# One decoder trunk on one core: seven quarter products in place of eight for the attention's queries and keys, too

## The reference, cut to what matters

```python
h = rms_norm(x, norm_mix[l])
proj = h @ w_in[l]                       # (256 x 1024) @ (1024 x 3584)
hq, hf, hi, hgate, aq, ak, av = jnp.split(proj, IN_SPLITS, axis=-1)   # 512 columns each
y_hg = hgrn2_mixer(hq, hf, hi, hgate, lbs[l], hg_out_norm[l])
y_att = dilated_attention_mixer(aq, ak, av, positions)
#   in it: qh = rope(heads(q), positions) * ATT_DH ** -0.5; kh = rope(heads(k), positions)
#   rope: concatenate([t1 * cos - t2 * sin, t2 * cos + t1 * sin]) of the halves t1, t2 of each head
x = x + jnp.concatenate([y_hg, y_att], axis=-1) @ w_out[l]
x = x + memory_cross_attention(rms_norm(x, norm_cross[l]), rms_norm(mem, norm_mem[l]), wq_x[l], wkv_x[l], wo_x[l])
x = x + hierarchical_moe(rms_norm(x, norm_ffn[l]), ...)
```

## Time and profile before

| | us |
|---|---|
| median of 3 runs (lowest, highest) | 1067.57 (1065.05, 1068.66) |
| the profiled execution | 1068.05 |
| its span | 1065.8 |
| TensorE busy (share of the span) | 1024.3 (96%) |
| VectorE busy | 413.5 (39%) |
| ScalarE busy | 135.6 (13%) |
| GpSimd busy | 98.4 (9%) |
| DMA, mean rate over the span | 275 GB/s |

### The profile page before, as it was taken

How to read it: one execution, slowest core, us unless ns; L and a number is a source line. 1 busy time by engine, 2 the same in 40 slices (tenths; PEclk the granted TensorE clock), 3 DMA queues, 4 the chain that set the end, 5 groups by cost and what they waited for, 6 DMA issues and landing times.

```text
span 1065.8 us, 10641 instructions
## 1 busy us (share of the span) xinstructions
PE 1024.3 (96%) x4360; PEld 549.1 (52%) x4360; DVE 413.5 (39%) x734; ACT 135.6 (13%) x307; POOL 98.4 (9%) x123
## 2 busy tenths in 40 slices
PE   6999999999998999999999999999999999999996
PEld 5757556567564543333333855565864433333332
DVE  2523375622143243332443636473032434444433
ACT  2211001412010011001112000041020011111111
POOL 2051032000001000000000512210000100000000
PEclk9999999999999999999999999999999999999999
DMA  9943001954038899999999520078463699999994
GB/s 359 424 175 141 17 0 69 417 229 157 1 158 339 353 395 422 415 423 421 418 422 419 223 79 1 0 305 346 162 237 123 241 422 421 421 421 421 421 422 179
DMA packets 43673, 293.58 MB, mean 275 GB/s; under 512 B 5344, under 2 KB 5600, under 8 KB 10848
## 3 DMA queue, kind: packets, MB, share of 16 engines
q1 hardware_dynamic: 36848, 266.35, 61.3%
q10 hardware_dynamic: 5616, 22.24, 5.3%
q0 software_dynamic: 1152, 4.19, 1.0%
HBM read 283.33 MB, written 9.44 MB: 275 GB/s over the span
## 4 chain that ended last, share of the span: by engine, by line
PE 89%; DVE 3%; DMA 3%; ACT 1%; SPq 1%; issue 1%; POOL 0%; DVEq 0%; POOLq 0%; ACTq 0%
PE bank L879 19%; PE bank L707 10%; PE bank L935 10%; PE bank L528 9%; PE bank L518 8%; PE bank L546 5%; PE bank L548 5%; PE bank L940 5%; PE bank L614 5%; PE bank L636 3%; DMA ring<-in_w_experts 3%; PE bank L508 2%; SPq L469 1%; PE bank L759 1%; PE bank L772 1%; PE bank L788 1%
## 5 line engine op out<-in xcount | busy, mean ns | idle before, releaser
L879 PE MATMUL bank<-ring,hT 128*64 128x512 f32 x704 | 182.8, 594 | 0.1
L707 PE MATMUL bank<-ring,hT 128*128 128x512 f32 x256 | 112.1, 594 | 0.0
L879 PEld LDWEIGHTS bank<-ring,hT 128*64 128x64 f32 x704 | 57.8, 137 | 93.8 <-issue 92.8
L528 PE MATMUL bank<-hT,ring 128*128 128x256 f32 x448 | 97.4, 379 | 0.8 <-DVE hT L1431 0.8
L1725 DVE TENSOR_TENSOR x<-bank,x 128x512 f32<-128x512 f32 x64 | 44.3, 692 | 137.5 <-PE bank L940 137.5
L528 PEld LDWEIGHTS bank<-hT,ring 128*128 128x128 f32 x448 | 84.9, 190 | 12.8 <-issue 1.4
L518 PE MATMUL bank<-ring,hT 128*128 128x512 f32 x192 | 84.4, 592 | 0.0
L707 PEld LDWEIGHTS bank<-ring,hT 128*128 128x128 f32 x256 | 48.0, 190 | 57.7 <-issue 56.8
L935 PE MATMUL bank<-ring,Vx 128*64 128x512 f32 x208 | 58.0, 596 | 2.7 <-ACT Vx L1167 2.4
L940 PE MATMUL bank<-PT 128*128 128x512 f32 x128 | 59.2, 605 | 0.0
L935 PE MATMUL bank<-ring,work 128*64 128x512 f32 x256 | 56.8, 596 | 2.2 <-ACT work L1167 2.2
(11 more groups left out here) (270 smaller groups left out, 1294.4 us busy)
## 6 DMA issues: line engine op xcount, KB each, us to landing
ring<-in_w_experts SPq DMA_DIRECT2D x160, 1024.0 KB, 13.9
ring<-in_w_mix SPq DMA_DIRECT2D x60, 1024.0 KB, 16.3
late<-in_w_experts SPq DMA_DIRECT2D x12, 1024.0 KB, 20.8
keys<-in_w_experts SPq DMA_DIRECT2D x10, 1024.0 KB, 20.4
work<-in_w_experts SPq DMA_DIRECT2D x10, 1024.0 KB, 24.1
late<-in_w_mix ACTq DMA_DIRECT2D x4, 2048.0 KB, 11.1
rot<-by_slot ACTq DMA_DIRECT2D x14, 512.0 KB, 8.0
by_slot<-late ACTq DMA_DIRECT2D x1, 4096.0 KB, 38.7
```

Source lines behind the costliest of these rows:

```text
L528: last = nc.tensor.matmul(b[:, k * T:(k + 1) * T], w[:, c, (n2 + k) * P:(n2 + k + 1) * P], rhs[:, c, :], start=(c == 0), stop=(c == C - 1))
L707: last = nc.tensor.matmul(held[name[1:], n, m][:, :], hT[:, c, m * P:(m + 1) * P], w[:, c, :], start=(c == 0), stop=(c == C - 1))
L879: last = nc.tensor.matmul(banks[2 + g][b2 * CAP:(b2 + 1) * CAP, :], rows_T_of(p)[:, c, b2 * CAP:(b2 + 1) * CAP], w, start=(c == 0), stop=( ...
```

## The change: what it does

aq and ak are computed by seven quarter products n1 to n7, with the same sums of rows as m1 to m7. m4 moves from behind the levels into the filling of level 4, with n1. GpSimd forms m4's weights in one subtraction of 128x2048 ahead of the levels; behind m5 it forms two more sums (in the slot SUMS, whose last use is now n4) and a third behind level 0's product of K, and n4's weights in pieces behind the products of levels 4 and 5's index (two pieces each). ScalarE copies n1 twice. VectorE adds the others into `rot` in SBUF and rotates there: `rotate` reads SBUF in place of the banks, sines first. The rotations end in the order of `TURNS`, and so go the transposes; s0 waits for qT1 in place of kT1.

```diff
+TURNS = [("qT", 0), ("kT", 1), ("kT", 0), ("qT", 1)]
 FIRST_SEVENTHS = [("m1", "A"), ("m2", "D")]
-BETWEEN = [[("m6", "D"), ("m5", "D")], [("m7", "D"), ("m3", "D")], [("hg0", "D")], [("hg1", "D")],
-           [("aq0", "D")], [("aq1", "D")], [("ak0", "D")], [("ak1", "D")]]
+BETWEEN = [[("m6", "D"), ("m5", "D")], [("m7", "D"), ("m3", "D")], [("hg0", "D")], [("hg1", "D")], [("m4", "D"), ("n1", "A")],
+           [("n2", "D"), ("n6", "D")], [("n5", "D"), ("n7", "D")], [("n3", "D"), ("n4", "D")]]
...
-    jobs += [("m4", "D")] + [(f"{name}{m}", "A") for name in ("qT", "kT") for m in range(M)]
+    jobs += [(f"{name}{m}", "A") for name, m in TURNS]
...
-LAST_USE = {"hf": "hf1", "hq": "hq1", "hi": "m4", "av": "m3", SUMS: "m5", "aq": "aq1", "ak": "ak1", "hg": "hg1",
+LAST_USE = {"hf": "hf1", "hq": "hq1", "hi": "m4", "av": "m3", SUMS: "n4", "aq": "n4", "ak": "n3", "hg": "hg1",
...
                 def seventh(name):
+                    one, two, late_sums = ("hi", "av", 4) if name[0] == "m" else ("aq", "ak", 11)
+                    t = 0 if name[0] == "m" else 4
                     rows_at, sums_at, weights, weights_at = {
+                        "1": (rows_block(0, 0), 0, weight_block(L, one, 0), 0), "2": (rows_block(0, 1), 0, weight_block(L, one, 1), 0),
+                        "5": (token_sums(0), 1, weight_block(L, SUMS, 0), t + 1), "6": (token_sums(1), 2, weight_block(L, SUMS, 1), t + 2),
+                        "7": (token_sums(2), 3, weight_block(L, two, 0), t + 3), "3": (token_sums(3), 4, weight_block(L, two, 1), 0),
+                        "4": (rows_block(1, 1), 0, weight_block(L, one, 0), late_sums)}[name[1]]
...
-                seventh("m4")
-                for w, name in enumerate(("qT", "kT")):
-                    for m in range(M):
-                        pe.wait_ge(rot_done, 4 * L + 2 * w + m + 1)
...
+                for i, (name, m) in enumerate(TURNS):
+                    pe.wait_ge(rot_done, 4 * L + i + 1)
+                    rr = turned(("qT", "kT").index(name), m)
+                    transposes(L, f"{name}{m}", [rr[:, k * P:(k + 1) * P] for k in range(4)])
...
+                wait_job(act, L, "n1")
+                nc.scalar.activation(turned(0, 1), bank("n1")[:, :], ACT.Copy)
+                empty("n1", turned(0, 0))
...
+                wait_job(pool, L, "m1")
+                weight_sums(minus(b11, b21, t2, ALU.subtract))
+                pool.wait_ge(weight_sum, 11 * L + 4)
+                c11, c21, c12, c22 = (weight_block(L, name, k) for name in ("aq", "ak") for k in range(2))
...
+                wait_job(pool, L, "m5")
+                weight_sums(minus(t1, c12, c11, ALU.subtract))
+                pool.wait_ge(weight_sum, 11 * L + 5)
+                weight_sums(minus(t2, c22, t1, ALU.subtract))
+                pool.wait_ge(weight_sum, 11 * L + 6)
                 for j in range(7):
...
-                    if 1 <= j <= 4:
-                        wait_job(pool, L, "m1")
-                        weight_sums(minus(b11[:, j - 1, :], b21[:, j - 1, :], t2[:, j - 1, :], ALU.subtract))
+                    if j == 0:
+                        weight_sums(minus(c12, c22, c12, ALU.subtract))
+                        pool.wait_ge(weight_sum, 11 * L + 7)
+                    if j in (4, 5):
+                        wait_job(pool, L, "n1")
+                        for c in (2 * j - 8, 2 * j - 7):
+                            weight_sums(minus(c11[:, c, :], c21[:, c, :], t2[:, c, :], ALU.subtract))
...
                 def rotate(w, m):
-                    name = f"{('aq', 'ak')[w]}{m}"
-                    wait_job(dve, L, name)
-                    t = bank(name)[:, :].rearrange("p (h u i) -> p h u i", u=2, i=32)
...
-                    V.tensor_tensor(r, t, cs, ALU.mult)
-                    emptied(V.tensor_tensor(b, t, sn, ALU.mult))
-                    wait_emptied(dve, L, name)
+                    link(V.tensor_tensor(b, r, sn, ALU.mult))
+                    link(V.tensor_tensor(r, r, cs, ALU.mult))
                     V.tensor_tensor(r[:, :, 0, :], r[:, :, 0, :], b[:, :, 1, :], ALU.subtract)
                     V.tensor_tensor(r[:, :, 1, :], r[:, :, 1, :], b[:, :, 0, :], ALU.add).then_inc(rot_done, 1)
...
+                def sum_seventh(name):
+                    of = name[0]
+                    one0, two0, one1, two1 = (hi[:, 0, :], av[:, 0, :], hi[:, 1, :], av[:, 1, :]) if of == "m" else \
+                        (turned(0, 0), turned(1, 0), turned(0, 1), turned(1, 1))
+                    if name[1] == "2":
+                        emptied(add_seventh(name, one0, one0, of + "1"))
+                        ready = (0, 0)
...
+                    elif name[1] == "7":
+                        add_seventh(name, two1, two0, of + "5")
+                        emptied(add_seventh(name, one1, one1, of + "6"))
+                        ready = (1, 1)
+                    elif name[1] == "3":
+                        emptied(add_seventh(name, two0, two0, of + "7"))
+                        ready = (1, 0)
+                    else:
+                        emptied(add_seventh(name, one1, one1, of + "7"))
+                        ready = (0, 1)
+                    if of == "n" and ready:
+                        wait_emptied(dve, L, name)
+                        rotate(*ready)
...
                 for j, some in enumerate(BETWEEN):
+                    for name, _ in some:
+                        if name[:2] == "hg":
+                            gate(int(name[2]))
+                        elif name != "n1":
+                            sum_seventh(name)
...
-                emptied(add_seventh("m4", hi[:, 1, :], hi[:, 1, :], "m7"))
                 wait_job(dve, L, "cross")
```

More of the change, by code:

```diff
@@ L597, in seventh @@
                 def seventh(name):
+                    one, two, late_sums = ("hi", "av", 4) if name[0] == "m" else ("aq", "ak", 11)
+                    t = 0 if name[0] == "m" else 4
                     rows_at, sums_at, weights, weights_at = {
[L600 to L607, removed]
+                        "1": (rows_block(0, 0), 0, weight_block(L, one, 0), 0), "2": (rows_block(0, 1), 0, weight_block(L, one, 1), 0),
+                        "5": (token_sums(0), 1, weight_block(L, SUMS, 0), t + 1), "6": (token_sums(1), 2, weight_block(L, SUMS, 1), t + 2),
+                        "7": (token_sums(2), 3, weight_block(L, two, 0), t + 3), "3": (token_sums(3), 4, weight_block(L, two, 1), 0),
+                        "4": (rows_block(1, 1), 0, weight_block(L, one, 0), late_sums)}[name[1]]
+                    if name[1] in "12":
+                        wait_loaded(pe, L, one, int(name[1]) - 1)
+                    if name[1] == "3":
+                        wait_unit(L, two)
                     if sums_at:
@@ L716, in _ @@
                 outputs = [(n, m) for m in range(M) for n in range(2)]
-                wait_emptied(pe, L, "kT1")
+                wait_emptied(pe, L, "qT1")
                 for k in range(3):
@@ L1098, in _ @@
                     nc.scalar.activation(gg[:, m, :], bank(f"hg{m}")[:, :], ACT.Exp, scale=-1.0).then_inc(gate_exp, 1)
[L1099 to L1102, removed]
+                wait_job(act, L, "n1")
+                nc.scalar.activation(turned(0, 1), bank("n1")[:, :], ACT.Copy)
+                empty("n1", turned(0, 0))
+                for name, m in TURNS:
+                    w = ("qT", "kT").index(name)
+                    empty(f"{name}{m}", attT[:, 4 * w:4 * w + 4, m * P:(m + 1) * P], scale=(DH ** -0.5 if w == 0 else 1.0),
+                          view=bank(f"{name}{m}")[:, :].rearrange("p (g t) -> p g t", t=P))
                 for m in range(M):
@@ L1278, in _ @@
                     pool.wait_ge(tot_done, 6 * L + tot_n)
+                wait_job(pool, L, "m1")
+                weight_sums(minus(b11, b21, t2, ALU.subtract))
+                pool.wait_ge(weight_sum, 11 * L + 4)
+                c11, c21, c12, c22 = (weight_block(L, name, k) for name in ("aq", "ak") for k in range(2))
+                for half in range(2):
+                    wait_loaded(pool, L, "aq", half)
+                    wait_loaded(pool, L, "ak", half)
+                wait_job(pool, L, "m5")
[3 more added lines that the diff above has]
+                pool.wait_ge(weight_sum, 11 * L + 6)
                 for j in range(7):
@@ L1490, in _ @@
                 tj = [F] + tots
[L1491 to L1504 removed]
+                def sum_seventh(name):
[5 more added lines that the diff above has]
+                        ready = (0, 0)
+                    elif name[1] == "6":
+                        emptied(add_seventh(name, one1, one1, of + "1"))
+                        ready = None
+                    elif name[1] == "5":
+                        emptied(add_seventh(name, two0, one1, of + "6"))
+                        ready = None
+                    elif name[1] == "7":
[11 more added lines that the diff above has]
+                        rotate(*ready)
```

31 lines of the change are left out of this document (10 added, 21 removed).

## The result

The kernel after takes 1072.93 us (median of 9 runs, 1070.26 to 1075.06), against 1067.57 of the kernel before (9 runs, 1064.98 to 1068.66). The ratio is 1.0049, with an interval from 1.0037 to 1.0062: slower by about 5.2 us (the medians lie 5.36 apart). The forecast was 1071.4, 3.8 us slower; the sign and the place are right, the size is 1.5 us short. 1072.93 lies 0.3 us above the forecast's own range of 1070 to 1072.6 and, as a number, nearer to rival C's 1074 than to the forecast.

What follows compares the result with a forecast made beforehand. TensorE bounds nearly the whole span, DMA the end; VectorE becomes last at cross. Per layer 166.67 + 13.5 + 2.4 + 0.4 + 0.07, plus 0.83, gives 183.9 against 182.02; 1067.57 + 3.8 = 1071.4 us, range 1070 to 1072.6 (8 in 10: 1062.5 to 1075.5).

Steps and rivals of the forecast that it cites:

- rival C: More waits: level 2's second half waits too, port turns worse at levels 5 to 7; 3.2 us per layer, 1074; chance 0.12.
- TensorE's saving: aq and ak by seven quarter products: 3.44 us less between level 7 and the transposes, 6.9 us in two layers without waits.
- VectorE's queue from n7: From n7's end to level 7's last product VectorE has no idle time: 13.5 us, so it arrives last at cross.
- Turns of the ports: VectorE operations with two SBUF inputs and GpSimd operations don't overlap, each waits for the other; bank reads are free of it.
- First sums: GpSimd's two subtractions behind m5 hold up VectorE's products of Q; level 1's second half waits: +0.83 us, bounds 0 to 1.2.
- Third sum: GpSimd's subtraction behind level 0's product holds VectorE's product for level 1; cost 0, up to 0.3 without the 0.6 us cover.
- n4's pieces: Pieces behind level 5's products delay VectorE's four rotation operations, 2.4 us with GpSimd's products (bounds 0 to 3.4); n4 waits 0.8.
- At cross: Cross, TensorE's product behind the transposes, starts at 183.9 against 182.02: +1.9 us per layer, twice that 3.8.
- A: The saving comes through: VectorE isn't the bound and the blocking is hidden; 1060.7 us; chance 0.12.
- B: VectorE's queue is as added up but GpSimd costs it little: -1.7 us per layer, 1064.2 us; chance 0.18.
- D: Later release of q0's to p1's slots makes the cross attention's first output product wait; price 0, chance nil.
- Behind "cross" the order is the old one: After cross its copy, the squares and the roots follow by the same distances; no slack to give back, no further change.

Runs made afterwards that it cites:

- e6: Kernel after, fillings reordered (n1 n2, n6 n5, n7 n3, n4 m4), all GpSimd sums in 128x512 pieces spread behind the first five products of K: 1060.90 us, ratio 0.9941.
- e9: Kernel after without GpSimd's four new sums; n4 to n7 take the weights' blocks as they stand, so aq and ak aren't the reference's: 1066.44 us, ratio 1.0005.
- e7: Kernel before with only the GpSimd program of the kernel after, its results unused, aq and ak plain: 1068.11 us, ratio 1.0010.
- e1: Kernel after with all four pieces of n4's sum behind level 4's product of K, none behind level 5's: 1068.06 us, ratio 1.0008.
- e5: Kernel after, fillings reordered to n1 n2, n6 n5, n7 n3, n4 m4, n4's four pieces behind level 4's product; large sums stay: 1061.51 us, ratio 0.9941.
- e10: Kernel before with GpSimd's new program, results unused, and ScalarE copying aq's and ak's banks to SBUF, where VectorE rotates: 1067.57 us, ratio 1.0017.
- e3: Kernel after with large sums in 128x512 pieces behind the first three products of K and n4's four pieces behind level 4's: 1067.77 us, ratio 0.9999.
- e2: Kernel after with the three sums of 128x2048 cut into 128x512 pieces, four behind each of the first three products of K: 1068.79 us, ratio 1.0019.
- e4: Kernel after with idle products in TensorE's waits, seven ahead of the last transposes and six ahead of cross: 1071.52 us, ratio 1.0035.
- e8: e3 with idle products in TensorE's waits, two ahead of the last transposes and six ahead of cross: 1065.87 us, ratio 0.9988.

## Why the prediction was right, and where it was short

- **TensorE's saving** (6.9 us if nothing waits): shown by e6, 3.36 and 3.43 of 3.44 us in the distances, and 6.4 us in the median.
- **VectorE's queue from n7** (13.5 us by itself): with GpSimd's products of K alone it measured 14.38 us (e9), with the pieces 16.14 (kernel after). The prediction has 13.5 and 0.4, and the 2.4 us of which 0.5 are turns with products of K if I read its waits of 0.1 and 0.4 so: 14.4, and 16.3 in all. (The four waits that it lists add up to 2.5 and not to 2.4, and e9's expectation had the 0.5 only in part.)
- **Turns of the ports.** First sums: 0.83 forecast, 0.85 measured, and alone in e7 0.93 in the distance, with the 0.10 of the longer job. Third sum: cost 0 forecast; 4.49 us of VectorE's product beside it and no wait. n4's pieces: 2.0 of VectorE's time and a wait of 0.8 at n4 forecast; measured 0.70 at n4, and taking the pieces away (e1) gave 1.85 at cross.
- **At cross:** +1.9 per layer forecast, +1.8 measured. So the forecast holds by its mechanism, term by term. The conditions of rivals A and B appear only where the order or the sums are changed (e5 and e6 for A; e9 for B, which gave -0.92 per layer and not B's -1.7). C's number is nearer to the measured one, but C's cause isn't there: level 2's second half didn't wait, and the turns at levels 5 to 7 came as added up. D didn't come either: no product waits for q0.
- **The step that was short** is "Behind "cross" the order is the old one ... by the same distances". The order is the old one, but from cross to the first scores the profiled execution took 1.58 us more in one layer and 0.17 in the other. 1.41 of it comes with the lower clock behind the waits, in that layer alone; 0.15 to 0.18 is there in every layer of all kernels with the new jobs that kept its clock. Together with the distances (2 x 1.8) that makes 5.35 us, against 5.36 between the medians. That they meet so closely is luck: the other stretches of that execution add -0.55, and the opening alone varies by 4 us.
- **Where the 0.17 us come from.** 0.10 is in cross (1.16 us for 1.06), 0.07 in the ten records behind it. In all kernels that have it, e5 and e6 too, cross starts 0.05 to 0.08 us behind the end of VectorE's last product; in e7 and e10, which don't have it, that product ends over 1.2 us ahead (at 180.97 for a cross at 183.55, at 178.23 for 179.47). So it goes with a cross that VectorE releases at the last moment. Why that makes it longer no run shows.
- What stays open: why one layer of an execution loses the clock and the other not, behind the same waits.

## What to carry to other kernels

When work leaves the engine that is full, add up the queue of the engine that gets it, in its order, from the last moment at which its input is there to the point where somebody waits; a busy share of half says nothing about it. Put the heaviest pieces of such a queue in early fillings and a light one last. Where GpSimd shares the time with VectorE, cut its instructions small and place them beside VectorE's reads from banks or its idle time; the first two operations of a rotation moved from a bank to SBUF are as long by themselves (0.69 us) and no longer independent of GpSimd (0.99 beside its product).

## What the runs showed of the hardware

- The kernel after has waits of 1.7 and 1.4 us on TensorE close together, and in one layer they were followed by a granted clock of 0.72 over 6 us. In one layer each of e1, e3 and e9 waits of 0.7 to 0.8 and 1.4 us were followed by the same 0.72 (5.39 to 5.40 us from cross to scores, against 3.99). Of the ten layers with both waits in the profiled executions of after, e1, e2, e3 and e9 four lost the clock; of the four with idle products in the waits (e4, e8) none did, and none of the ten without them (before, e5, e6, e7, e10). Four layers alone could be chance; the mean clocks of all runs under e4 and e8 speak for the filling. e2 had the long waits and kept the clock in its profiled execution; two of its others, at 1073.2 and 1073.3 us, have a mean clock of 0.990 and 0.991, and where it fell there isn't on record. A lost layer costs 1.4 us.
- VectorE and GpSimd take turns instruction by instruction when both queue: a waiting one goes next, whichever engine had the ports (pieces back to back took 3.00 us for two of 1.27 with VectorE's operations between). A masked copy from a bank (COPY_PREDICATED, mask in SBUF) is not held up: 0.73 us beside e3's pieces at 137.99.
- A level's second half and cross are 0.10 us longer when a VectorE product releases them at the last moment (1.16 us for 1.06), with a wait that the trace records or, in e5 and e6, without one.
